# Small vectors loaded as rows, eight multiply-adds a unit, probabilities scaled on ScalarE

## The reference

```
cond = silu(c)
h = x
for layer in 0, 1:
    sh1, sc1, g1, sh2, sc2, g2 = split(cond @ w_ada[layer] + b_ada[layer], 6)
    u = rms_norm(h, norm_mix[layer]) * (1 + sc1) + sh1
    if layer == 0:
        q, k, v, bg, cg, xv = split(u @ w_in)        # 512, 128, 128, 512, 512, 512 wide
        attn = sliding_window_attention(q, k, v, sinks)   # 8 heads of 64, 2 kv heads, window 128, ALiBi
        conv = bg * causal_depthwise_conv3(cg * xv, conv_w)
        mix = concat(attn, conv) @ w_out
    else:
        mix = multiscale_pool_mixer(u, w_pool, pool_scale)
    h = h + g1 * mix
    u = rms_norm(h, norm_ffn[layer]) * (1 + sc2) + sh2
    h = h + g2 * grouped_moe(u, w_router, b_router, ...)  # 16 experts, top 2 in the best of 4 groups
return rms_norm(h, norm_final)
```

## Time and profile before

| | us |
|---|---|
| median of 3 runs | 781.47 (779.27 to 781.55) |
| profiled execution, its own time | 773.66 |
| its span, first to last instruction | 771.8 |
| TensorE (PE) busy | 670.5 (87%) |
| VectorE (DVE) busy | 346.4 (45%) |
| ScalarE (ACT) busy | 167.4 (22%) |
| GpSimd (POOL) busy | 120.9 (16%) |

### The profile page before, as it was taken

How to read it: one execution, slowest core, us unless ns; L and a number is a source line. 1 busy time by engine, 2 the same in 40 slices (tenths; PEclk the granted TensorE clock), 3 DMA queues, 4 the chain that set the end, 5 groups by cost and what they waited for, 6 DMA issues and landing times. The chain is left out here.

```text
span 771.8 us, 7170 instructions
## 1 busy us (share of the span) xinstructions
PE 670.5 (87%) x2437; PEld 351.9 (46%) x2437; DVE 346.4 (45%) x623; ACT 167.4 (22%) x422; POOL 120.9 (16%) x97
## 2 busy tenths in 40 slices
PE   5996999999699974999999999479399999999970
PEld 3453444444344463454554554169255545554530
DVE  4125699899961445422322322336643223223222
ACT  5000312212322321211221221145022212211212
POOL 0030001001030032022122121200101221222120
PEclk9997999999799965999999999879589999999995
DMA  9989989978780466497898892199715889988416
GB/s 344 384 218 362 367 307 331 335 265 300 263 304 0 164 230 261 164 342 299 299 354 320 302 343 53 28 389 372 280 33 220 338 316 323 333 331 306 150 24 233
DMA packets 56010, 204.27 MB, mean 265 GB/s; under 512 B 9686, under 2 KB 18942, under 8 KB 43692
## 3 DMA queue, kind: packets, MB, share of 16 engines
q1 hardware_dynamic: 45012, 183.62, 62.2%
q0 software_dynamic: 10432, 19.55, 11.1%
q10 hardware_dynamic: 536, 0.73, 0.3%
HBM read 193.06 MB, written 27.30 MB: 286 GB/s over the span
## 5 line engine op out<-in xcount | busy, mean ns | idle before, releaser
L1552 PE MATMUL ps<-ring,work 128*128 128x512 f32 x384 | 169.0, 593 | 0.3 <-ACT work L755 0.3
L1552 PEld LDWEIGHTS ps<-ring,work 128*128 128x128 f32 x384 | 72.8, 190 | 90.5 <-issue 89.9
L852 DVE SCALAR_TENSOR_TENSOR acc<-adaw,cond,acc 128x1024 f32<-128x1024 f32 x70 | 96.1, 1373 | 19.1 <-DMA adaw<-in_w_ada_dram 17.3
L550 POOL DMA_INDIRECT h_dram<-work x32 | 51.7, 1614 | 299.9 <-DVE work L1167 291.3
L1148 DVE TENSOR_TENSOR work<-work,ps 128x256 f32<-128x256 f32 x32 | 13.5, 422 | 177.8 <-ACT work L761 177.8
L1575 PE MATMUL psY<-ring,work 128*128 128x512 f32 x192 | 86.6, 594 | 1.2 <-ACT work L771 1.2
L1404 PE MATMUL psY<-xu,ring 128*128 128x512 f32 x192 | 85.2, 596 | 0.0
L1167 DVE SCALAR_TENSOR_TENSOR work<-psY,work,gbc 128x512 f32<-128x512 f32 x64 | 45.1, 747 | 74.4 <-PE psY L1575 74.4
L761 ACT ACTIVATE work<-ps 128x256 f32<-128x256 f32 x32 | 12.3, 383 | 271.1 <-PE ps L1552 271.1
L755 ACT ACTIVATE work<-psA,modc,scl 128x128 f32<-128x128 f32 x120 | 45.1, 456 | 51.4 <-PE psA L1542 51.4
L1552 PE MATMUL ps<-xu,work 128*128 128x512 f32 x128 | 56.2, 592 | 0.0
(11 more groups left out here) (189 smaller groups left out, 640.1 us busy)
## 6 DMA issues: line engine op xcount, KB each, us to landing
adaw<-in_w_ada_dram SPq DMA_DIRECT2D x84, 512.0 KB, 5.5
ring<-in_w_gate_dram SPq DMA_DIRECT2D x24, 1024.0 KB, 5.0
ring<-in_w_up_dram SPq DMA_DIRECT2D x24, 1024.0 KB, 7.6
ring<-in_w_down_dram SPq DMA_DIRECT2D x24, 1024.0 KB, 11.7
xu<-in_w_gate_dram SPq DMA_DIRECT2D x8, 1024.0 KB, 5.2
xu<-in_w_up_dram SPq DMA_DIRECT2D x8, 1024.0 KB, 7.5
xu<-in_w_down_dram SPq DMA_DIRECT2D x8, 1024.0 KB, 11.4
work<-in_w_ada_dram SPq DMA_DIRECT2D x12, 512.0 KB, 9.1
```

What stands on the lines that cost most here:

```text
L550: pool.indirect_dma_start(out=h_dram[l], out_offset=bass.IndirectOffsetOnAxis(tok_i[:, e:e + 1], 0), in_=yrow[:, e % 2, :], in_offset=None ...
L852: dve.scalar_tensor_tensor(total, adaw[:, n % ABUF, :], cond[:, k:k + 1], total if k else brow[:, :], ALU.mult, ALU.add).then_inc(mac_step, 1)
L1552: ins = pe.matmul(gu_ps[j % 2][:, :].rearrange("p (a f) -> p a f", a=2), xgT[:, j % 2, k, :], w_gu(j % 4)[:, :, k, :], start=(k == 0), sto ...
```

## The change

Sinks come in one load and are put in order on VectorE. `conv_w` and both `norm_mix` come as rows in `vrow`, which TensorE turns. `PLACES` has 5 and 15 multiply-adds at the first two places instead of 8 and 12, then eight a unit instead of nine, seven in unit 6 instead of six and five in unit 7 instead of none. ScalarE scales the probabilities in `share(u)`, four instructions a unit, after its first evictions of the unit.

```diff
-        N_SMALL = 10
+        N_SMALL = 5
+        V_MIX, V_CONV, V_ROWS = 2 * KD, 4 * KD, 4 * KD + 3 * CC
...
-        PLACES = [8, 12] + [3] * 18 + [2, 2, 2] + [0] * 6
+        PLACES = [5, 15] + [3, 3, 2] * 6 + [3, 2, 2, 2, 2, 1] + [0] * 3
...
-                return NPC if i == len(PLACES) - 1 else sum(PLACES[:i - LAG + 1]) // KD
+                return NPC if i == len(PLACES) - 1 else max(1, sum(PLACES[:i - LAG + 1]) // KD)
...
-            for kv in range(KVH):
-                for odd in range(2):
-                    src = sinks[:, kv * GH + odd:(kv + 1) * GH:2].partition_broadcast(P).rearrange("p a e -> p (a e)")
-                    pool.dma_start(snk[:, 0, kv * GH + 2 * odd:kv * GH + 2 * odd + 2], src).then_inc(small_in, 16)
-            pool.dma_start(cvw[:, :, :], conv_w[0].rearrange("j (c p) -> p j c", p=P)).then_inc(small_in, 16)
+            pool.dma_start(snk[:, 1, :], sinks.partition_broadcast(P).rearrange("p a e -> p (a e)")
+                           ).then_inc(small_in, 16)
...
-            for s in range(1, 4):
-                src = (norm_ffn if s % 2 else norm_mix)[s // 2]
-                src = src.rearrange("(k p) -> p k", p=P) if s == 2 else src.rearrange("(p k) -> p k", k=KD)
-                pool.dma_start(normc[:, s, :], src).then_inc(small_in, 16)
+            for s in (1, 3):
+                pool.dma_start(normc[:, s, :], norm_ffn[s // 2].rearrange("(p k) -> p k", k=KD)
+                               ).then_inc(small_in, 16)
             load_gate(0, 0)
-            for u in range(ATT_U):
-                b = u // KVH
-                pool.wait_ge(rden_ready, u + 1)
-                lo = 0 if b else P
-                part = prob[:, u % 2, :, lo:]
-                pool.tensor_tensor(part, part, sm[:, u % 2, 4, :].unsqueeze(2).broadcast_to([P, GH, 256 - lo]),
-                                   ALU.mult).then_inc(prob_ready, 1)
...
-            act.dma_start(vrow[2 * KD:3 * KD, :], norm_mix[0:1].rearrange("a (r n) -> (a r) n", n=P)
+            act.dma_start(vrow[V_MIX:V_CONV, :], norm_mix.rearrange("l (r n) -> (l r) n", n=P)).then_inc(vrow_in, 16)
+            act.dma_start(vrow[V_CONV:V_ROWS, :], conv_w[0].rearrange("j (c n) -> (j c) n", n=P)
                           ).then_inc(vrow_in, 16)
...
+            def share(u):
+                act.wait_ge(rden_ready, u + 1)
+                lo = 0 if u // KVH else P
+                for g in range(GH):
+                    ins = act.activation(prob[:, u % 2, g, lo:], prob[:, u % 2, g, lo:], ACT.Copy,
+                                         scale=sm[:, u % 2, 4, g:g + 1])
+                ins.then_inc(prob_ready, 1)
...
                 for m in BESIDE[u][0]:
                     empty(m)
+                if u < ATT_U:
+                    share(u)
                 if u and u % KVH == 0:
                     empty_att(u // KVH - 1)
...
-                link(dve.tensor_copy(normc[:, 0, :], ps4[:, 32 + 2 * KD:32 + 3 * KD]))
+                dve.tensor_copy(cvw[:, :, :], ps4[:, 32 + V_CONV:32 + V_ROWS].rearrange("p (j c) -> p j c", j=3))
+                link(dve.tensor_copy(normc[:, 0:3:2, :],
+                                     ps4[:, 32 + V_MIX:32 + V_CONV].rearrange("p (l k) -> p l k", l=2)))
...
             dve.wait_ge(small_in, 16 * N_SMALL)
+            link(dve.tensor_copy(snk[:, 0, :].rearrange("p (v o i) -> p v o i", v=KVH, o=2),
+                                 snk[:, 1, :].rearrange("p (v i o) -> p v o i", v=KVH, o=2)))
...
-            pe.wait_ge(vrow_in, 32)
-            pe.transpose(ps4[:, 32:32 + 3 * KD], vrow[0:3 * KD, :], ident[0:3 * KD, 0:3 * KD]).then_inc(vcol_banked, 1)
+            pe.wait_ge(vrow_in, 48)
+            pe.transpose(ps4[:, 32:32 + V_ROWS], vrow[0:V_ROWS, :], ident[0:V_ROWS, 0:V_ROWS]).then_inc(vcol_banked, 1)
```

## The result

The changed kernel takes 759.85 us (median; 758.21 to 765.68 in four runs) against 781.51 in the same comparison: ratio 0.974, 95% interval 0.968 to 0.980. The forecast was 766.7, with a range of 759 to 774.5. In the profiled executions the span goes from 771.8 to 757.5 us.

What follows compares the result with a forecast made beforehand. TensorE, busy 87% of the span, was taken as the bound, so only its standstills and half clock counted; +0.7 - 10.1 - 1.6 - 4.2 + 0.4 = -14.8 us gave 758.9 profiled, 766.7 as median, range 759 to 774.5.

Steps and rivals of the forecast that it cites:

- start: Before the first product, the added rows delay loading and transposing: +0.7 us, bounds 0.3 and +9.
- first products, wait and clock: Near 63 us, fewer small loads and five multiply-adds ahead remove TensorE's standstill and its half clock: -10.1 us.
- unit 5, wait: At `turn_prob(5)` in attention, TensorE's wait for probabilities shrinks from 6.82 to 2.9 us: -3.9 us.
- unit 5, clock: After the `turn_prob(5)` wait, half of the 2.9 us lost to the lower clock comes back: -1.4 us.
- unit 5, wait for `w_out`: At `mix_half(0)`, 3 MB of output weights issued after multiply-add 58 land too late: +1.1 us (0 to 3).
- tail: In unit 8, the last sum's tile is turned after the last `mix_half(2)`, hiding all but +0.4 us.
- rival D: At the start, added rows land 9 us later and delay the whole chain: 775.0 us, chance 0.05.
- Rival A: Front stall stays in part, only 3.9 of 10.1 us come: 772.9 us, chance 0.15.
- The collision: In attention units, VectorE's multiply-adds are lengthened beside GpSimd's multiply; moving the scaling returns 1.5 us a unit.
- rival C: In attention, ScalarE's queue becomes the chain and makes every `turn_prob` late: slower, 794.3 us, chance 0.04.
- The offset: Whole kernel: timed median lies 7.8 us above the profiled execution; the prediction added this to its profiled result.
- Rival B: In unit 5, VectorE's freedom also removes the clock loss and the `w_out` wait: 761.3 us, chance 0.10.

Runs made afterwards that it cites:

- e10_filler: Changed kernel plus one unread 512-column matmul after each of the eight groups of router logits; 765.31 us, ratio 0.982 to the kernel before.
- e2_rows: Kernel before with only the small vectors loaded as rows and the sinks in one load; 772.37 us, ratio 0.9918.
- e5_no_share: Changed kernel, but GpSimd still scales the probabilities; 764.53 us, ratio 0.9811 to the kernel before.
- e8_later: Changed kernel with multiply-adds moved out of units 5 and 6 to later places and late `w_out` load at n = 62; 762.1 us, ratio 0.977.
- e9_conv_back: Changed kernel with one `conv_w` load put back on GpSimd's queue into a tile nobody reads; 764.57 us, ratio 0.981 to the kernel before.
- e11_rest_back: Changed kernel with three sink loads and `norm_mix[1]` put back on GpSimd's queue, unread; 775.61 us, ratio 0.994 to the kernel before.
- e4_no_rows: Changed kernel, but small vectors still loaded element by element; 775.5 us, ratio 0.9955 to the kernel before.
- e3_share: Kernel before with only the scaling of probabilities moved from GpSimd to ScalarE; 772.55 us, ratio 0.9938.
- e7_unit5: Changed kernel with multiply-adds of units 4, 5 and 7 rearranged and late `w_out` load at n = 62; 761.4 us, ratio 0.979 to the kernel before.
- e6_no_places: Changed kernel, but with the old `PLACES` (8 and 12, nine a unit); 765.21 us, ratio 0.9826 to the kernel before.

## Why the prediction was right, and where it was not

Term by term (us), "after" from the changed kernel's profile, "e10" from the second execution of its code:

| term | forecast | after | e10 |
|---|---|---|---|
| start | +0.7 | +0.41 | +0.49 |
| first products, wait and clock | -10.1 | -10.27 | -8.88 |
| two small waits for probabilities | -1.6 | -1.6 | -1.6 |
| unit 5, wait | -3.9 | -4.47 | -4.47 |
| unit 5, clock | -1.4 | -2.8 | -1.2 |
| unit 5, wait for `w_out` | +1.1 | 0 | 0 |
| wait before `mix_half(1, 0)` | 0 | -0.70 | -0.70 |
| wait of the sum near 100 us | 0 | +0.85 | +1.94 |
| tail | +0.4 | 0 | 0 |
| sum; measured at `mix_half(3, 0)` | -14.8 | -18.6; -18.41 | -14.4; -14.26 |

**The start.** The transpose of 44 rows starts at 9.37 us instead of 9.08; the added rows did not land late, and rival D is out. It is not always as little: over the nine profiles with the rows the first product starts at 22.84 to 23.12 us in five and at 23.63 to 23.71 in four (e2_rows, e5_no_share, e8_later, e9_conv_back, with the transpose at 10.04 to 10.12), against 22.35 to 22.54 in the five without.

**The first products** came whole, by the mechanism named: e2_rows shows that rows alone take the wait away, e11_rest_back that small loads alone undo the traffic. The reason given for the size, four fifths of the elements, did not hold: `conv_w` has 1,536 of the 3,584 and costs 0.4 us (e9_conv_back), and by the packets it was three sink loads, 768 elements. And the prediction priced the small loads at this wait alone; place 1 hangs on the same transfers, and that is where e4_no_rows and e11_rest_back lose most. Rival A, a stall that stays in part, did not come in the changed kernel. That the whole 10.1 us came was in part luck, as the size was taken from the wrong count.

**Unit 5, wait.** 2.35 us stay, 2.9 forecast. Half of the difference is that the four scalings took 1.71 us and not 2.0. The ScalarE page of the Trainium skill (ScalarE: Activation LUTs, What ACT_TABLE_LOAD costs), from whose figures the prediction had worked out 1.7, agrees with the trace.

**Unit 5, clock.** Half of the 2.9 us was counted as lost. The changed kernel's profile lost none, and by it alone this step would read as wrong. Six other profiles of versions with such a wait lost 1.6, one of them of the same code, so the step was right.

**Unit 5, `w_out`.** This step failed, by a misreading of the code and not of the machine. I took 1 MB as loaded at n = 40 and 3 MB at n = 64, and it is the other way round; the text ahead of the prediction has the same error. The 13.2 us of the earlier trace rows belong to the load at n = 40, long in place. The late one is 1 MB and lands in 6.0 us, and no wait came.

```profile
ring<-in_w_out_dram SPq DMA_DIRECT2D x1, 3072.0 KB, 12.0
...
ring<-in_w_out_dram SPq DMA_DIRECT2D x1, 1024.0 KB, 6.0
```

**Other waits.** Not foreseen were the wait of a sum in unit 1, 0.85 us at 99.30 and 1.94 in e10_filler (place 1 with 15 multiply-adds makes that piece late), and that the 0.70 us before `mix_half(1, 0)` went. The tail's 0.4 did not show: `mix_half(3, 0)` waits 1.86 us, before 1.85. The last sum moved into that stretch, so the stretches of the first table read -3.67 and +0.99.

**The collision** of VectorE with GpSimd is real: in e3_share, which changes nothing else on VectorE, a multiply-add takes 1,284 ns instead of 1,400, 54 x 0.116 = 6.3 us over the stage. That is 0.8 us a unit; the 1.5 us that the prediction read from one unit is more than most of them lost. ScalarE's queue did not become the chain (rival C): `turn_prob` waits for it once.

**The offset.** The prediction put the 7.8 us between profile and median onto its result, taking the profile's sum as typical. That was sound in kind: most of them lie behind `mix_half(3, 0)`, where the profile of before was quick. The forecast, 766.7, is 6.9 us above the median. 1.5 of that are the misread `w_out` and the tail; the rest is no more than what separates two profiled executions of the same code, and what decides where an execution loses its clock is not settled here. That the sum of -14.8 stands so near e10_filler's -14.3 is luck too: its errors run from -1.1 to +1.9 us and cancel. The timed gain, 16 to 25 us, is larger than either. Rival B (761.3) named the right size for it, by a loss of clock that only the one profile is free of.

## What to carry to other kernels

Where an engine waits for data in a slice with a fifth of its neighbours' GB/s and the DMA engines still half busy, look at the small loads in flight, and at their packets before their elements: here loads of the sinks, 1 KB each, slowed the weights, and one of 1,536 single elements did not. Try the cure with the rest of a change as well as alone, since here it was worth 6.4 us alone and 16.9 (at least 10, by the intervals) among the others. Work moved off one wait in a queue without slack shows up at the next (e7_unit5, e8_later). And a profile of the changed kernel is one draw: compare it with a second of the same code before a term of the sum is called wrong.

## What the hardware did that was not expected

- The same 128 logits matmuls of 16 moving columns took 17.0 to 22.7 us in thirteen profiles, by where the granted clock fell; with wide matmuls between them it stayed up in all of layer 1 in one more.
- The clock can be at its lower level in the first products too: between 21 and 31 us it was granted at 1.00 in the profile of the changed kernel and at 0.62 to 0.86 in those of e2_rows, e6_no_places and e7_unit5, which cost up to 3 us, with no wait to show for it.
- A wait of 2.35 us was followed by 1.6 us of loss at the lower clock in four profiles and by none in a fifth.
- Small loads of like size differ more than tenfold in what they cost the large ones: 0.4 us at place 0 for the 6 KB of e9_conv_back, 6.5 for the 7 KB of e11_rest_back. A packet of 64 bytes of sinks took 1.13 to 1.17 us, one of 512 bytes of the router's bias 0.03.
